# Attention of a two-layer decoder step: another order of loads and stores on one DMA queue

## What is computed

```python
kv = (_rmsnorm(h, kv_norm) @ w_kv).reshape(B, S, 3, 2, 4, 128)     # cmp, slc, win; keys, values
proj = _rmsnorm(h, norms_l[0]) @ w_q_l                             # q and the gates
p_c = _attn_probs(q, ckv[:, :, 0], ...)                            # compressed past
o_c = einsum('bhgqk,bkhd->bqhgd', p_c, ckv[:, :, 1])
o_s = sel_fn(q, sel)        # selected blocks: here all of them; sample: pages of cache_slc_kv + new rows
o_w = win_fn(q)             # window: sample: state_win_kv + new rows
o = gates[:, :, 0] * o_c + gates[:, :, 1] * o_s + gates[:, :, 2] * o_w
h = h + _rmsnorm(o.reshape(B, S, 2048) @ w_o_l, norms_l[1])        # output projection
h = _ffn_sublayer(h, norms_l, w_in, w_out)
# among the outputs: y, and the new key and value rows (kv) of every branch
```

## Time and profile before

| | us |
|---|---|
| median of 3 runs | 2634.51 |
| lowest and highest run | 2634.45, 2635.32 |
| the profiled execution, its own time | 2629.14 |
| its span in the trace | 2627.5 |

### The profile page before, as it was taken

One profiled execution on the slowest core, in us unless ns is written; L12 is line 12 of the kernel. 1 busy time (PEld: TensorE's weight loads), 2 busy tenths in 40 slices (PEclk: granted clock), 3 DMA queues, 4 the chain that ended last, 5 costly groups with the idle time before them and its releaser, 6 DMA issues.

```text
span 2627.5 us, 44090 instructions
## 1 busy us (share of the span) xinstructions
PE 2540.3 (97%) x17340; PEld 2484.0 (95%) x17340; DVE 1212.5 (46%) x1372; ACT 913.5 (35%) x1130; POOL 291.6 (11%) x324
## 2 busy tenths in 40 slices
PE   8799999999999999999999789999999999999997
PEld 6799999999999999999997579899999999999997
DVE  6564444444444444643434544644444444444444
ACT  3354333323322333532324443533233233323332
POOL 2430000000000001300002221300000000000012
PEclk9899999999999999999999899999999999999999
DMA  6524444444444444445445534334444444444443
GB/s 250 177 96 146 155 162 145 153 152 158 157 146 163 153 144 149 139 157 175 158 177 163 164 128 144 128 135 144 159 159 152 148 162 153 135 166 162 144 151 128
DMA packets 88810, 403.36 MB, mean 154 GB/s; under 512 B 13245, under 2 KB 23885, under 8 KB 58931
## 3 DMA queue, kind: packets, MB, share of 16 engines
q1 hardware_dynamic: 82594, 390.06, 43.5%
q0 software_dynamic: 6160, 12.60, 1.5%
HBM read 394.88 MB, written 19.02 MB: 158 GB/s over the span
## 4 chain that ended last, share of the span: by engine, by line
PE 85%; DVE 5%; ACT 3%; SPq 3%; DMA 2%; issue 2%; POOL 0%; DVEq 0%; ACTq 0%
PE ps L1285 27%; PE ps L1286 27%; PE ps L1287 27%; ACT w_hi L477 1%; DMA pastK<-win_k_dram 1%; SPq L361 1%; DVE w_lo L740 1%; PE ps L1376 1%; PE ps L1463 1%; DVE winB L847 1%; DVE winA L847 0%; ACT y L585 0%; ACT x_hi L503 0%; PE ps L1549 0%; PE ps L1608 0%
## 5 line engine op out<-in xcount | busy, mean ns | idle before, releaser
L1285 PE MATMUL ps<-x_hi,w_hi 128*128 128x320 f32 x3536 | 1095.1, 310 | 7.6 <-DVE sg L911 4.1
L1287 PE MATMUL ps<-x_hi,w_lo 128*128 128x320 f32 x3536 | 1093.1, 309 | 0.0
L1286 PE MATMUL ps<-x_lo,w_hi 128*128 128x320 f32 x3536 | 1093.1, 309 | 0.0
L740 DVE TENSOR_TENSOR w_lo<-w_raw,w_hi 128x2048 fp32r<-128x2048 f32 (+1 forms) x364 | 749.0, 2058 | 654.3 <-ACT w_hi L477 654.3
L477 ACT CAST w_hi<-w_raw 128x2048 fp32r<-128x2048 f32 (+1 forms) x364 | 623.2, 1712 | 534.0 <-PE ps L1287 475.3
L1285 PEld LDWEIGHTS ps<-x_hi,w_hi 128*128 128x128 f32 x3536 | 664.2, 188 | 9.9 <-DVE sg L911 4.6
L1286 PEld LDWEIGHTS ps<-x_lo,w_hi 128*128 128x128 f32 x3536 | 664.2, 188 | 0.4 <-issue 0.2
L1287 PEld LDWEIGHTS ps<-x_hi,w_lo 128*128 128x128 f32 x3536 | 664.1, 188 | 0.0
L1287 PE MATMUL ps<-hid_hi,w_lo 128*128 128x320 f32 x1408 | 435.1, 309 | 0.0
L1285 PE MATMUL ps<-hid_hi,w_hi 128*128 128x320 f32 x1408 | 435.1, 309 | 0.0
L1286 PE MATMUL ps<-hid_lo,w_hi 128*128 128x320 f32 x1408 | 435.1, 309 | 0.0
(11 more groups left out here) (234 smaller groups left out, 1529.6 us busy)
## 6 DMA issues: line engine op xcount, KB each, us to landing
w_raw<-w_in_dram SPq DMA_DIRECT2D x176, 1024.0 KB, 4.9
w_raw<-w_out_dram SPq DMA_DIRECT2D x128, 704.0 KB, 4.0
w_raw<-w_kv_dram SPq DMA_DIRECT2D x24, 1024.0 KB, 6.2
w_raw<-w_q_dram SPq DMA_DIRECT2D x17, 1024.0 KB, 4.9
w_raw<-w_o_dram SPq DMA_DIRECT2D x15, 1024.0 KB, 4.9
win_out_dram<-win_kv_dram POOLq DMA_DIRECT2D x8, 992.0 KB, 5.2
rowsK<-cmp_data_dram SPq DMA_DIRECT2D x16, 256.0 KB, 9.3
w_raw<-w_pool_dram SPq DMA_DIRECT2D x4, 1024.0 KB, 7.1
```

Of the source, the lines that this page charges most:

```text
L740: V.tensor_tensor(w_lo[:, slot, 0:width], src, w_hi[:, slot, 0:width].bitcast(F32), ALU.subtract).then_inc(lo_made, 1)
L1285: M(out, wh, xh[:, k, :], start=(k == 0), stop=False)
L1286: M(out, wh, xl[:, k, :], start=False, stop=False)
L1287: last = M(out, wl, xh[:, k, :], start=False, stop=(k == kt - 1))
```

## The change

Three things move on SyncE's queue, and nothing on another engine. The keys of sample `b + 1` are asked for ahead of the values of sample `b`. The eight stores leave the loop over samples and stand behind panels 2 to 9 of the output projection. The loop over the panels 2 to 15, which ran with a register, is written out.

```diff
-        for b in range(DB):
-            load_keys(b)
+        load_keys(0)
+        load_values(0)
+        sp.wait_ge(crow_sum, 2)
+        panel(P_WO, 0, w_o[0], PW)
+        load_keys(1)
+        for b in range(1, DB):
+            if b < DB - 1:
+                load_keys(b + 1)
             load_values(b)
-            part = slice(b * N_KVT // DB, (b + 1) * N_KVT // DB)
-            sp.dma_start(kv_out[:, part, :], kvT[:, part, :]).then_inc(rows_out, 16)
-            if b == 0:
-                sp.wait_ge(crow_sum, 2)
-                panel(P_WO, 0, w_o[0], PW)
             if b == DB // 2:
                 sp.wait_ge(s_made, place(PW // NT) + 1)
                 sp.dma_start(w_rawY[:, :], w_o[1]).then_inc(raw_in[(P_WO + 1) % 2], 16)
 
-        with sp.Fori(1, KT // 2) as i:
-            for j in range(2):
-                panel(P_WO + j, i, w_o[i * 2 + j], PW)
+        for i in range(2, KT):
+            panel(P_WO + i, 0, w_o[i], PW)
+            if i < DB + 2:
+                part = slice((i - 2) * N_KVT // DB, (i - 1) * N_KVT // DB)
+                sp.dma_start(kv_out[:, part, :], kvT[:, part, :]).then_inc(rows_out, 16)
```

## The result

| | before, us | changed, us |
|---|---|---|
| median | 2634.48 (4 runs, 2633.53 to 2635.32) | 2597.96 (4 runs, 2595.23 to 2599.88) |
| traced execution | 2629.14 | 2597.47 |

The ratio of changed to before is 0.9861, 95% interval 0.9844 to 0.9878: 36.5 us faster. The forecast was 2603.1, range 2599.5 to 2612.5.

A forecast was written before the change was run, and what follows sets the result against it. TensorE's 22.3 us of waits for past keys, and the slow clock behind them, bound the kernel. Six periods falling from 114.55 to 83.1 us gain 31.45: 2629.14 to 2597.7, plus 5.4 offset, 2603.1 us; range 2599.5 to 2612.5.

The forecast's parts named there:

- the wait and its place: Attention: TensorE's score matmuls wait for past keys in six of eight samples, 22.3 us, keys queued behind values and store.
- Keys and values: Load queue: keys land 7.1 us after the release (keys' buffer free); last values leave at 6.4 us at the latest.
- the cover: Time between the keys' landing and TensorE's need of them: 1.7 to 4.6 us, taken as 4.6.
- Rival 2: Attention: value loads wait out the keys' transfer, land 2.2 us late; period 16.05, time 2616.3 us; chance 0.07.
- The period: Attention, from one release to the next, two prompt heads and a sample: 13.85 us without the wait.
- the softmax chain's hold: Attention: VectorE, ScalarE and GpSimd work between scores and transposes holds TensorE 0.1 us once a period.
- The clock: TensorE in attention: falls only behind the stall, 1.00 without it; some 9 us of the gain.
- The stores and the panel for the second buffer: Output projection and load queue: moved stores and the panel `w_rawY` delay nothing needed, cost 0.
- the last one of the sum: Whole kernel: median stays 5.4 us above the traced execution, carried from 2597.7 to 2603.1 us.
- The sum itself: Six attention periods fall from 114.55 to 83.1 us, gain 31.45 us.

The follow-up runs named there:

- E3: Against the kernel before: next sample's keys loaded ahead of the values, output panels written out, stores left in the loop over samples; median 2598.91 us, ratio 0.9874.
- e4: Against the kernel before: stores moved behind the output projection's panels, old order of values then keys kept; median 2615.27 us, ratio 0.9935.
- E5: Kernel before with its old queue, plus 14 or 24 needless small matmuls ahead of the wait for keys of samples 2 to 7; median 2621.38 us, ratio 0.9967.
- E2: The changed kernel, unedited, measured and traced once more, on another run of the kernel before's chip; median 2597.38 us, ratio 0.9868.
- E1: The kernel before, unedited, measured and traced once more; median 2633.61 us, traced execution 2634.25 us.

## Why the prediction missed by 1.5 us

**What bounds the kernel, the wait and its place: right.** All six waits went. E3 shows that the place of the keys in the queue is enough for the whole gain. It does not show that the stores were worth nothing in the kernel before: moved alone they give 16.6 us (e4), of the same wait. The written-out loop over the panels stood in e3 and e4 too and was not run alone.

**Keys and values: right.** From release to landing the keys took 1420.82 - 1418.16 + 4.1 = 6.8 us, forecast 7.1; the cover was 4.9, forecast 4.6. The last value DMA left 5.6 us after the release, forecast 6.4 at the latest, and landed at most 4.9 us later, 10.5 us after the release, and was needed at 14.9 (line 1611 at 1433.04). Rival 2, the values as the new wait, never came near.

**The period: mechanism right, 0.18 us too long.** The forecast's 11.73 us from release to the next scores ran from 1418.77 to 1430.50, and so already held the 0.20 us of the softmax chain's hold; 0.1 was added for it once more, and the starts of two matmul groups overlap by 0.07 us. In six periods that is 1.1 us.

**The clock: right,** 1.00 in all six periods. By the traces of before and after, the 32.55 us of gain in the six periods are 22.3 of wait and 11.2 of slow work (92.05 - 80.86), less 1.0 of short holds by GpSimd's scaling: the changed kernel has one of 0.19 us in each period, the kernel before only in the first. That leaves 10.2 for the clock and the holds together, forecast 9. E5 shows that the clock has a price apart from the wait; its 9.7 us are what it costs beside a stall that stays, so they are no second measurement of the same sum.

**The stores and the panel for the second buffer: right,** cost 0. In the changed kernel the casts of the output projection are 7.04 us apart while stores run (the casts at 1541.55 and 1548.59), as before. E2, with the same stores in the projection, takes 1074.8 us from the first output tile to the end, the kernel before 1074.9.

**The step that failed is the last one of the sum: "The median shown, 2634.51, is 5.4 us above that execution, and I carry the offset."** The 5.4 us were treated as something that stays. E1 shows that they are in what the change removes: an execution at 2634.25 has six periods of 119.18 us, the one of 2629.14 has 114.55. These are two traces, no more, but the scatter says the same: 12.9 us in 29 runs with the stall, 4.7 in eight without. The four runs of the kernel before in the result lay within 1.8 us and did not let this be seen. The stall is made of DMA landings (5.0 to 6.9 us in the two traces) and of a clock that falls for a varying time, and these scatter; the periods without a wait were 13.66 or 13.67 us in every trace. The offset should have been dropped: 2629.14 - 31.45 = 2597.7, against 2597.96 measured. The sum itself met its own trace, though partly by luck, since 2.3, 1.7 and 1.5 us in untouched parts nearly cancelled. The range was drawn around the wrong centre and had its room on the other side, for rivals that did not come.

## What to carry to other kernels

On a queue that works in order, put ahead what becomes free first and is needed first; here that alone gave all of the gain, and the load that stood behind a wait for another buffer made TensorE wait 3 to 6 us a round. A long stall of TensorE costs its length and the slow clock behind it, here half as much again. Two changes that shorten the same wait do not add up: one of them was worth 16.6 us alone and nothing behind the other. When the trace of a kernel is faster or slower than its median, ask whether the difference sits in the very thing that the change removes: then it goes with it. Here the kernel freed of its stalls had less scatter as well as a lower time.

## What was not expected of the hardware

- The clock fell to its lower level behind a wait of 1.87 us and not behind waits of 1.50 and 1.67 (e4), and behind the same 1.72 us wait in one execution of the changed kernel and not in another (13.83 against 12.17 us for the same work).
- The kernel with the stalls scattered over 2625.4 to 2638.4 us on one chip (29 runs), the changed kernel over 2595.2 to 2599.9 us (eight runs, two measurements).
- A 1.97 MB store put ahead of a load delayed its landing by 3.4 us, where 5.8 were put down for the store's transfer: it was under way (246 GB/s) while the queue was still reading page numbers and issuing.
- A 480 KB store between the values and the keys did not make the keys land later after their issue (5.0 to 6.9 us with it, 4.8 to 7.2 without), but with it the two paged loads took 2.6 to 2.9 us to issue at five of six samples of the first trace, and 1.9 at all six of e4 without it.
